# A two-block decoder stack on one core: mask, scale and row maximum of the attention logits in one Vector instruction per half of the queries

## The reference, cut to what matters

```
logits = einsum('bhqd,bhkd->bhqk', qb, k) * scale        # fox: + dq - log_decay_cum
logits = where(k_pos <= q_pos, logits, -inf)             # dilated: + log(how many patterns reach the key)
p      = softmax(logits, axis=-1)
out    = einsum('bhqk,bhkd->bhqd', p, v)
```

## Time and profile before

| | us |
|---|---|
| median of 3 runs | 1964.96 |
| lowest and highest | 1963.36, 1968.75 |
| the profiled execution | 1963.63 |
| its span in the trace | 1961.7 |
| PE busy | 1884.0 (96%) |
| DVE busy | 1467.0 (75%) |
| ACT busy | 1141.5 (58%) |
| POOL busy | 39.4 (2%) |

### The profile page before, as it was taken

The page is one execution under the profiler, slowest core; times in us unless marked ns, Lnnn a source line. Parts: engine busy times, 40 slices in busy tenths (PEclk is TensorE's granted clock), DMA queues, the critical chain, the costliest instruction groups (busy, mean ns, idle before and its releaser), DMA issues.

```text
span 1961.7 us, 28126 instructions
## 1 busy us (share of the span) xinstructions
PE 1884.0 (96%) x11217; PEld 1635.8 (83%) x11217; DVE 1467.0 (75%) x1543; ACT 1141.5 (58%) x1239; POOL 39.4 (2%) x84
## 2 busy tenths in 40 slices
PE   7879999999999899999999999999999999899998
PEld 6758889999976788888888888888888887899997
DVE  4677746555644498988989889888898897697685
ACT  5532234334343476767767667677776776566653
POOL 0020000000012000000000000000000000000010
PEclk9999989999987799999999999999999999999999
DMA  7200034554420488988889889899898998443441
GB/s 323 86 1 1 1 129 172 182 183 174 149 87 1 188 361 341 369 349 348 359 335 374 352 347 353 343 368 356 340 368 328 371 355 331 181 146 134 156 146 43
DMA packets 64208, 467.44 MB, mean 238 GB/s; under 512 B 7248, under 2 KB 7376, under 8 KB 7888
## 3 DMA queue, kind: packets, MB, share of 16 engines
q1 hardware_dynamic: 64080, 465.66, 61.3%
HBM read 464.58 MB, written 1.05 MB: 237 GB/s over the span
## 4 chain that ended last, share of the span: by engine, by line
PE 87%; DVE 7%; ACT 3%; issue 2%; DMA 1%; POOL 0%; SPq 0%; DVEq 0%; ACTq 0%
PE bank L551 85%; PE bank L561 3%; DVE split_ring L1872 1%; ACT arena L1340 1%; ACT split_ring L1340 1%; DVE arena L1903 0%; ACT L1340 0%; DMA weight_ring<-w_dram 0%; DVE arena L2587 0%; DVE arena L1904 0%; ACT moe_pair_high L1340 0%; ACT operand_high L1340 0%; ACT late_high L1340 0%; POOL arena L2679 0%; DVE arena L1882 0%
## 5 line engine op out<-in xcount | busy, mean ns | idle before, releaser
L2433 DVE TENSOR_TENSOR moe_pair_low<-weight_ring,moe_pair_high 128x2048 fp32r<-128x2048 f32 x225 | 507.2, 2287 | 15.8 <-ACT moe_pair_high L1340 15.2
L1340 ACT ACTIVATE moe_pair_high<-weight_ring 128x2048 fp32r<-128x2048 f32 x225 | 427.0, 1917 | 39.1 <-DMA weight_ring<-w_dram 37.9
L551 PE MATMUL bank<-moe_pair_high,operand_high 128*128 128x512 f32 x896 | 353.6, 395 | 3.5 <-DVE operand_low L2440 2.5
L551 PE MATMUL bank<-moe_pair_high,operand_low 128*128 128x512 f32 x896 | 352.3, 393 | 0.0
L551 PE MATMUL bank<-moe_pair_low,operand_high 128*128 128x512 f32 x896 | 349.9, 391 | 0.0
L551 PE MATMUL bank<-operand_high,split_ring 128*128 128x256 f32 x1536 | 328.6, 287 | 8.5 <-DVE split_ring L1872 8.2
L1340 ACT ACTIVATE arena<-bank 128x256 f32<-128x256 f32 (+4 forms) x209 | 90.4, 440 | 362.1 <-PE bank L551 326.8
L551 PEld LDWEIGHTS bank<-operand_high,split_ring 128*128 128x128 f32 x1536 | 256.5, 192 | 11.9 <-DVE split_ring L1872 9.6
L551 PEld LDWEIGHTS bank<-moe_pair_high,operand_high 128*128 128x128 f32 x896 | 168.7, 188 | 39.0 <-issue 2.7
L551 PEld LDWEIGHTS bank<-moe_pair_high,operand_low 128*128 128x128 f32 x896 | 168.4, 188 | 38.1
L551 PEld LDWEIGHTS bank<-moe_pair_low,operand_high 128*128 128x128 f32 x896 | 168.8, 188 | 36.7
(11 more groups left out here) (313 smaller groups left out, 3201.0 us busy)
## 6 DMA issues: line engine op xcount, KB each, us to landing
weight_ring<-w_dram SPq DMA_DIRECT2D x381, 1024.0 KB, 6.9
arena<-w_dram SPq DMA_DIRECT2D x55, 1024.0 KB, 4.9
constants<-const_dram SPq DMA_DIRECT2D x1, 3124.0 KB, 18.0
parameters<-param_dram SPq DMA_DIRECT2D x1, 2896.5 KB, 24.4
hT<-x_dram SPq DMA_DIRECT2D x1, 1024.0 KB, 4.9
out_dram<-squares SPq DMA_DIRECT2D x4, 256.0 KB, 2.1
constants<-const_dram SPq DMA_DIRECT2D x1, 128.0 KB, 4.7
parameters<-param_dram SPq DMA_DIRECT2D x1, 54.5 KB, 4.6
```

The lines of the kernel that those rows point to most:

```text
L551: return pe.matmul(out, lhsT, rhs, start=start, stop=stop, skip_group_check=True)
L1340: return act.activation(out, in_, f, **kw)
L2433: tt(low_, raw_, high_.bitcast(F32), ALU.subtract).then_inc(moe_split, 1)
```

## The change

The three DVE instructions per head are replaced. A new helper `lowest` issues a tensor_tensor_reduce: out = (bank + mask) x (-scale), and with it the minimum over the columns. It is called once per half of the queries (128 and 256 columns). The logits in SBUF are now negated, and their minimum is the negated row maximum, so `nmx` holds what it held. The exponentials take `scale=-1.0`. The mask of the dilated attention is multiplied by the square root of 64 on the host, since it is now added ahead of the scale; the causal mask is 0 or -1e30 and stays.

Each half counts `nmax_ready`, so ACT waits twice per head, and its first exponential may start when the first half is there. DVE waits for its own two instructions, and then a memset of one column frees the bank.

```diff
-    for name, m in (("causal", causal), ("dilated", dil)):
+    for name, m in (("causal", causal), ("dilated", dil * HD ** 0.5)):
...
-                        act.wait_ge(S["nmax_ready"], n + 1)
-                        st.lone(a_(Lg[i % NL][:, 0:P], Lg[i % NL][:, 0:P], ACT.Exp, bias=nmx[:, i, 0:1], accum_out=zsum[:, i, 0:1]))
-                        st.say(a_(Lg[i % NL][:, P:384], Lg[i % NL][:, P:384], ACT.Exp, bias=nmx[:, i, 1:2], accum_out=zsum[:, i, 1:2]), "exp_done")
+                        act.wait_ge(S["nmax_ready"], 2 * n + 1)
+                        st.lone(a_(Lg[i % NL][:, 0:P], Lg[i % NL][:, 0:P], ACT.Exp, scale=-1.0, bias=nmx[:, i, 0:1], accum_out=zsum[:, i, 0:1]))
+                        act.wait_ge(S["nmax_ready"], 2 * n + 2)
+                        st.say(a_(Lg[i % NL][:, P:384], Lg[i % NL][:, P:384], ACT.Exp, scale=-1.0, bias=nmx[:, i, 1:2], accum_out=zsum[:, i, 1:2]), "exp_done")
...
+            def lowest(out, raw, mask, scale, least):
+                return dve.tensor_tensor_reduce(out, raw, mask, -scale, 3e38, ALU.add, ALU.min, least)
...
-                        V.free(stt(Lg[i % NL], bank[:, 0:384], scale, m384, ALU.mult, ALU.add))
-                        dve.wait_ge(V.freed, V.nc)
-                        st.lone(dve.tensor_reduce(nmx[:, i, 0:1], Lg[i % NL][:, 0:P], AX_X, ALU.max, negate=True))
-                        st.say(dve.tensor_reduce(nmx[:, i, 1:2], Lg[i % NL][:, P:384], AX_X, ALU.max, negate=True), "nmax_ready")
+                        st.say(lowest(Lg[i % NL][:, 0:P], bank[:, 0:P], m384[:, 0:P], scale, nmx[:, i, 0:1]), "nmax_ready")
+                        st.say(lowest(Lg[i % NL][:, P:384], bank[:, P:384], m384[:, P:384], scale, nmx[:, i, 1:2]), "nmax_ready")
+                        st.wait_said("nmax_ready")
+                        V.free(dve.memset(tiny[:, 136:137], 0.0))
```

More of the change, by code:

```diff
@@ L1744, in exps @@
                 def exps(h):
-                    act.wait_ge(S["nmax_ready"], n0 + h + 1)
+                    act.wait_ge(S["nmax_ready"], 2 * (n0 + h) + 1)
                     L_ = late_Lg[h]
-                    st.lone(a_(L_[:, 0:P], L_[:, 0:P], ACT.Exp, bias=nmx[:, h, 0:1], accum_out=zsum[:, h, 0:1]))
-                    st.say(a_(L_[:, P:384], L_[:, P:384], ACT.Exp, bias=nmx[:, h, 1:2], accum_out=zsum[:, h, 1:2]), "exp_done")
+                    st.lone(a_(L_[:, 0:P], L_[:, 0:P], ACT.Exp, scale=-1.0, bias=nmx[:, h, 0:1], accum_out=zsum[:, h, 0:1]))
+                    act.wait_ge(S["nmax_ready"], 2 * (n0 + h) + 2)
+                    st.say(a_(L_[:, P:384], L_[:, P:384], ACT.Exp, scale=-1.0, bias=nmx[:, h, 1:2], accum_out=zsum[:, h, 1:2]), "exp_done")
                 def piece(c):
@@ L2517, in logits @@
                     bank = V.take(dve)
-                    V.free(stt(late_Lg[h], bank[:, 0:384], HD ** -0.5, m384, ALU.mult, ALU.add))
-                    dve.wait_ge(V.freed, V.nc)
-                    st.lone(dve.tensor_reduce(nmx[:, h, 0:1], late_Lg[h][:, 0:P], AX_X, ALU.max, negate=True))
-                    st.say(dve.tensor_reduce(nmx[:, h, 1:2], late_Lg[h][:, P:384], AX_X, ALU.max, negate=True), "nmax_ready")
+                    st.say(lowest(late_Lg[h][:, 0:P], bank[:, 0:P], m384[:, 0:P], HD ** -0.5, nmx[:, h, 0:1]), "nmax_ready")
+                    st.say(lowest(late_Lg[h][:, P:384], bank[:, P:384], m384[:, P:384], HD ** -0.5, nmx[:, h, 1:2]), "nmax_ready")
+                    st.wait_said("nmax_ready")
+                    V.free(dve.memset(tiny[:, 136:137], 0.0))
                 def norms(h):
```

## The result

| | before | after |
|---|---|---|
| median, us | 1964.59 (4 runs) | 1949.89 (4 runs) |
| lowest and highest | | 1949.18, 1954.96 |
| ratio after / before | | 0.9927, 95% interval 0.991 to 0.9944 |
| the profiled execution | 1963.63 | 1954.96 |
| its span | 1961.7 | 1953.0 |

The change gains 14.7 us. The forecast was 1962.7 us and the range ended at 1956.0: the prediction was wrong. The profiled execution of the changed kernel is the longest of its four, at a mean granted clock of 0.975 against 0.972 for the one of before; the other three lie at about 0.979. So the trace shows 8.7 us of the 14.7, and the rest is a clock that was higher still in the other executions.

What follows compares the result with a forecast made beforehand. PE was taken to bound the kernel (87% of the chain), DVE only in ten blocks. Gains of 1.6, 0.2 and 0.5 us in attentions 0 to 2 gave 2.3 us, so 1962.7 us; range 1956.0 to 1970.0 us.

Steps and rivals of the forecast that it cites:

- The blocks on the path: Ten of 40 head blocks on the chain of waits: seven in attention 0, one in attention 1, two in attention 2.
- no new stretching: POOL beside DVE: the new pass has one PSUM input like the old, so no added slowdown was expected.
- The cost of a block: DVE's work per head: passes, reads, wait and memset sum to 0.89 us against 1.12, a gain of 0.23 us.
- the cheap bound of 0.40: DVE block at its cheapest, reads and memset overlapping at a memset's duration each: 0.72 us, a gain of 0.40.
- Fixed costs eat the gain: Rival: nothing overlaps around DVE's new instructions, block 1.11 us, time stays at 1964.9 us; chance 0.21.
- the pace of a scan: Rival: DVE's new passes run as slowly as scans, block 1.53 us, ten blocks cost 4.1 us, 1969.1 us; chance 0.09.
- The clock stays up in attention 2: Rival: a shorter PE idle stretch ahead of 604.11 us avoids half clock, worth 6 us, 1956.7 us; chance 0.13.
- a clock that falls or rises elsewhere at another moment: Anywhere behind 120 us: the shift moves clock falls, both ways alike, no size given; chance 0.06.
- The signs of being wrong: DVE blocks and PE: a block longer than 1.12 us, or PE waiting for a freed V bank.
- the slower side: Rival: at a scan's pace the clock falls in attention 0, 1976.9 us, chance 0.07; slower than 1970.9 us: 0.10.

Runs made afterwards that it cites:

- before_filled: The kernel before, with head 3's scores in attention 2 computed four times to fill PE's idle stretch: 1960.82 us, ratio 0.9984.
- after_delayed: The changed kernel, with a 370-column memset on DVE behind each of the first two blocks of attention 2: 1955.11 us, ratio 0.9952.
- after_shift2: The changed kernel, with the last product of attention 0 on DVE done three times instead of once: 1961.88 us, ratio 0.9997.
- before_shift1: The kernel before, with the last product of attention 0 on DVE done twice: 1967.63 us, ratio 1.001.
- after_shift1: The changed kernel, with the last product of attention 0 on DVE done twice: 1959.22 us, ratio 0.9975.
- the 128 rows: Attention 1's decay matmuls over all 128 rows instead of 8: kernel before 1957.88 us; changed kernel 1948.13 us, run again 1945.91 us.

## Why the prediction was wrong, point by point

**The blocks on the path: right.** Seven, one and two of 40. Attention 1's step from the logits to POOL shrank by one block, attention 2's step to its first transposition by two, the late layers gave nothing. Attention 0 gave 2.4 us where seven blocks of 0.43 would be 3.0. Head 0 gained nothing, as counted: head 1's first pass waits 0.40 us for its scores. What the seven lack stands in the timeline. Two products between the heads last 1.33 and 1.28 us instead of 1.20, against the prediction's "no new stretching", and DVE stands still for 0.31 us ahead of head 7's first pass (132.87 us), for which the view names no releaser.

**The cost of a block: mis-sized.** The failed terms are the two reads and the memset: 0.09 + 0.18 + 0.03 + 0.06 = 0.36 us in the sum, measured 0.00 and 0.12 to 0.15 together. The passes were right (0.21 and 0.32 forecast, 0.21 and 0.35 measured). A block gains 0.43 us, which is even beyond the cheap bound of 0.40. That mis-sized the term by 0.20 us for each of ten blocks. I had taken ACT's accumulator read as the nearest row for DVE's; it isn't like it. With 0.43 the sum would have been 4.3 us, a median of 1960.7, still outside of what was measured.

**Fixed costs eat the gain, and the pace of a scan: both refuted** by the rows by shape: 286, 420 and 84 ns against 402 and 678 for scans. The last read does hold back the wait behind it, but an instruction that waits for nothing starts together with the read, at 125.85 us. The Trainium skill, VectorE: DVE Perf Modes, section "The DRAIN you can't avoid", has the next instruction wait for an empty pipe, and adds that one that is not held starts earlier. The prediction took only the first half. The trace agrees with the second for these instructions: 0.08 us of overlap between the pass and what follows it, and a read that costs 0.00 us between passes.

**The clock stays up in attention 2: it came, at the size forecast, but not for the reason given.** It was priced at 6 us and is 5.5 in the trace. Filling the idle stretch kept the clock up in the one trace of before_filled, and lengthening it brought the fall back in that of after_delayed. I gave the rival 0.13 because the idle gap would shrink only from 2.3 to 1.9 us; it shrank to 1.10. But the gap's length isn't what decides: with 1.09, 1.09, 1.13 and 1.30 us the clock fell in four other kernels. That the fall stayed away here is luck for this rival. Even with it and with blocks at 0.43 us, the sum ends at 1964.96 - 3.7 - 5.5 = 1955.8 us, 5.9 above the measured median.

**The step that failed is the range.** It ends at 1956.0 us, where the clock stays up in attention 2. It granted 0.06 to "a clock that falls or rises elsewhere at another moment", to both sides alike, and gave it no price. By the runs the clock, attention 2's and that elsewhere together, was the largest term of all: about 11 of the 14.7 us, which is what the path's 3.7 leave (the comparison at equal clock puts the path's part at 3.5). The mean granted clock went from 0.971 to 0.979. As 2 x (1 - clock) x time this is some 114 us at 1.2 GHz before and 82 after. The 32 us less would be worth 16 us were PE the bound in all of them. The number was there to be read: the profiled execution of the kernel before has a mean granted clock of 0.972, so that up to 0.028 x 1961.7 = 55 us hung on the clock over the whole span. The prediction looked at one stretch of it, 590 to 615 us at a clock of 0.57, where up to 0.43 x 20.89 = 9 us hung.

**The signs of being wrong did not show it.** They were a block longer than 1.12 us and a PE that waits for a freed V bank. The block is 0.68 us long, and no wait of PE for the memset stands in the waits of the changed kernel. Neither sign watched the clock elsewhere.

**Why the slower side stayed empty.** The clock holds in attention 0 of the changed kernel from 125 us on, as it did before the change. after_shift2 and before_shift1 show that the rival was real: with 2.4 and 1.2 us more of DVE work there the clock did fall in attention 0, at 134 and at 137 us. In after_shift1, with the same 1.2 us, it didn't.

**What stays open.** Which property of the moment decides a fall isn't settled. Shown is that the same code with the same idle gap keeps the clock or loses it when 1.2 to 2.4 us of work are added ahead of it, or when its start moves by as little as 0.3 to 0.5 us in the traces, and that single executions of one kernel differ in their mean clock. That the moment decides is the simplest reading of this, but no run moved the moment alone and repeated it in several traces. The Trainium skill, TensorE: Matmul & The Clock Gate, Part 1, says that the monitor behind the clock gate runs freely and isn't reset when a kernel starts; that fits what is seen here, but no run here proves it. Also open is how much of the 11 us would survive another edit upstream. With the same 1.2 us repeated on both sides (before_shift1 and after_shift1, measured on two chips) the change is worth 1967.63 - 1959.22 = 8.4 us; with the 128 rows on both sides it is worth 12.0; as it stands 14.7. Only the path's 3.7 us follow from the edit itself.

## What to carry to other kernels

A pass with its minimum, straight from PSUM, replaces scale, mask and maximum at less than two thirds of their time on DVE, and it pays only in the blocks that the chain of waits goes through. Where the granted clock is below 1.00 around an edit, price every low stretch behind it as well, as a term that can go to either side; here the clock was three times the path's gain. Before such a gain is counted as the edit's own, delay the kernel on purpose by a microsecond upstream and see what remains, and compare the executions of both kernels at equal granted clock.

## What the runs showed of the hardware

- The accumulator read on DVE lasts 84 ns and costs 0.00 us between two passes: the next pass starts with it (125.85 us for both). The read of the last pass and the wait behind it cost 0.12 to 0.15 us.
- A tensor_tensor_reduce with one input in PSUM lasts 286 ns for 128 columns and 420 ns for 256, and 0.21 and 0.35 us from start to start.
- The granted clock went to half at 572 and 574 us while PE was busy for 8.00 of 8.00 us, with matmuls over 8 of 128 rows among them. With all 128 rows it didn't fall there in three traces; in all 14 traces with 8 rows it fell between 566 and 577 us.
- It was 1.00 across gaps of 2.27 and 1.78 us in one kernel and fell behind gaps of 1.09 us in another.
- The executions of one and the same kernel ran from 1954.23 us at a mean granted clock of 0.978 to 1970.95 us at 0.968.
- 1.2 us of extra work on DVE cost 9.2 us in one kernel and, by the medians, 3.2 in another, and six extra matmuls in front of attention 2's first transposition made the kernel before no slower (by the medians 3.7 us shorter, the interval just reaching no change).
